# Whole instructions instead of quarters on GpSimd, in a two-layer mLSTM and attention trunk

## The chip, the cores and the metric

The kernel runs on 1 core of a Trainium2 chip. The core has five engines that work side by side: TensorE (PE, matrix products), VectorE (DVE), ScalarE (ACT), GpSimd (POOL) and SyncE (SP, which here only issues transfers). They meet only at semaphores. The metric is the device time of one execution in microseconds (us); lower is better.

## The reference, cut to what matters

Input and output are 1024 tokens of 1024 float32 numbers. Two layers are computed: layer 0 mixes tokens by an mLSTM with 4 heads in chunks of 128, layer 1 by differential attention with 8 heads. Each mixer and each MLP is preceded by an RMS norm and added to its input:

```
x = x + mixer_i(rmsnorm(x))              # i = 0: mLSTM, i = 1: differential attention
x = x + square(relu(rmsnorm(x) @ w_up)) @ w_down
out = rmsnorm(x)
# attention, per head, two maps c = 0, 1 with rotary q and k:
p_c = softmax(mask(q_c @ k_c.T * scale));  a = p_0 - lam * p_1;  o = a @ v
# rotary: concat(x1*cos - x2*sin, x2*cos + x1*sin)
```

## The kernel before, in words

Every product is done in three passes of a reduced-precision float32 (fp32r). A number v is split into a high part (v rounded to fp32r) and a low part (v minus the high part), and hi·hi + lo·hi + hi·lo are added up. So each weight panel of 1024x128 numbers must be split before PE may use it, and GpSimd does this for all panels of the mixers and of their output products: `split(g, slot, ...)` multiplies `w_raw` by ones into `w_hi` (the rounding), then subtracts into `w_lo`. There are 64 panels and two slots. The split of panel g starts when its weights are loaded and when PE has finished panel g-2 (`half_done`); PE waits for `w_split`, and SP waits for it before it loads the panel after next into the slot.

GpSimd has two more jobs of the same kind. `rotate(hd, j)` applies the rotary tables to q (j = 0) and k (j = 1) of an attention head: two products with sine and cosine tables and one sum over 128x1024 numbers. `split_early(layer)` splits finished mixer outputs (6 tiles of 128x1024 in layer 0, 7 in layer 1) while the last head is being computed, so that PE can begin the output product in between (`early_tile`). In these three functions each pass over 128x1024 numbers is issued as 4 instructions of 128x256 (the constant `PIECE` = 2 blocks of 128 columns). In the MLPs GpSimd runs `a_sums`, sums of weight blocks, each already one instruction of 128x1024; they are not touched.

The order of work on every engine is written out by hand. PE fills its waiting times in the mixers with the next panels' products: `feed(n)` issues n units of three matmuls between the steps of a head. In attention, step m of a head is: PE computes the scores (L1089, L1090), DVE adds the mask and takes the maximum for both maps (`mask_and_max`, L2148, L2149, both reading PSUM), ACT takes the exponentials (L1535), DVE combines the two maps (`combine`, L2160, which reads two SBUF tiles), and PE transposes the result (L1130) and multiplies it with v. Between the steps DVE also empties the panels' PSUM banks (`take`, L1649), and PE may overwrite a bank only after that. There are two banks, each used by every second half panel of 24 matmuls.

In the mLSTM DVE computes the gates of all heads in one long chain of small instructions (L1997 to L2017) while PE does the first panels. At each head's start it makes two tables (L2030, L2032), copies the new q, k and v (L2035, 128x4096) and prepares the decay matrix (L2039, L2043).

On the way from the first MLP to attention, SP issues the transfer that repeats q for the first head (`repeat_q`, L456, L459) behind a panel's load, and that load waits for the split of the panel before the last one (`load_panel`, L418).

Of the kernel before, what the change touches and what calls it, by code (L numbers as in the profile page):

```python
# [26 lines left out]
S = 1024  # L27
P = 128
NT = D // P
HALF = S // 2  # L30
# [8 lines left out]
NEG = -1e30  # L39


PIECE = 2
BATCHES = [-(-(m + 1) // 3) for m in range(NB)]
BEFORE = [sum(BATCHES[:m]) for m in range(NB)]
BATCH = sum(BATCHES)
# [60 lines left out]
def trunk(nc, x, ln_mix, ln_mlp, w_up, w_down, ln_f, m_w_in, m_b, m_norm, m_w_out,  # L106
          a_w_in, a_lam, a_norm, a_w_out, cos_t, sin_t, out):
    f32, f32r, i32 = mybir.dt.float32, mybir.dt.float32r, mybir.dt.int32
    ALU, ACT, AX = mybir.AluOpType, mybir.ActivationFunctionType, mybir.AxisListType
# [28 lines left out]
    def half_stage(layer, unit, s, q):  # L138

        return 2 * STAGES * UNITS * layer + 2 * stage_of(unit, s) + q + 1  # L140
# [66 lines left out]
    with ExitStack() as ctx:  # L207
        def sem(name):
            return ctx.enter_context(nc.semaphore(name))

        def sb(name, shape, dt=f32, stack=ctx):
            return stack.enter_context(nc.sbuf_tensor(name, shape, dt))


        h = sb("h", [P, NT, S])
# [7 lines left out]
        ones = sb("ones", [P, P])  # L223
# [13 lines left out]
        w_raw = sb("w_raw", [P, 2, NT, P])  # L237
        w_hi = sb("w_hi", [P, 2, NT, P], f32r)
        w_lo = sb("w_lo", [P, 2, NT, P], f32r)
# [34 lines left out]
        with ExitStack() as s:  # L274
# [8 lines left out]
            cosb = sb("cosb", [P, S], stack=s)  # L283
            sinb = sb("sinb", [P, S], stack=s)
# [74 lines left out]
        w_split = sem("w_split")  # L359
# [17 lines left out]
        y_early_hi, y_early = sem("y_early_hi"), sem("y_early")  # L377
# [6 lines left out]
        dve_chain, act_chain, pool_chain = sem("dve_chain"), sem("act_chain"), sem("pool_chain")  # L384
# [12 lines left out]
        pool_rot, rot_ready, qk_hi, qk_ready = sem("pool_rot"), sem("rot_ready"), sem("qk_hi"), sem("qk_ready")  # L397
# [232 lines left out]
        def _(pool):  # L630
# [16 lines left out]
            def split(g, slot, use, first=False):  # L647

                pool.wait_ge(w_ld[slot], 16 * use)
                if not first:  # L650
                    pool.wait_ge(half_done, 2 * (g - 1))
                if isinstance(g, int) and g in (G_MIX[1], G_MIX[1] + 1):

                    pool.wait_ge(hs_done, half_stage(0, UNITS - 1, 6, 0) - (1 if slot else 0))
                cuts = [slice(t, t + PIECE) for t in range(0, NT, PIECE)]
                for cut in cuts:
                    last = nc.gpsimd.tensor_tensor(w_hi[:, slot, cut], w_raw[:, slot, cut],  # L657
                                                   ones[:, :].unsqueeze(1).broadcast_to([P, PIECE, P]), ALU.mult)
                last.then_inc(pool_chain, 1)
                pool.wait_ge(pool_chain, 4 + g)  # L660
                for cut in cuts:
                    last = nc.gpsimd.tensor_tensor(w_lo[:, slot, cut], w_raw[:, slot, cut],  # L662
                                                   w_hi[:, slot, cut].bitcast(f32), ALU.subtract)
                last.then_inc(w_split, 1)


            split(1, 1, 1, first=True)

            for n in range(2, 2 * NT):
                pool.wait_ge(emit_hi, n + 1)  # L670
                if n >= 4:
                    pool.wait_ge(x_added, n - 3)
                nc.gpsimd.tensor_tensor(acc[:, n % 2], acc[:, n % 2], sq[:, n % 2], ALU.add).then_inc(x_added, 1)
            split(2, 0, 1)

            def pairs(start, end):

                with pool.Fori(0, (end - start) // 2) as i:
                    split(start + 2 * i, 1, i + (start + 1) // 2)
                    split(start + 1 + 2 * i, 0, i + (start + 1) // 2)  # L680

            def split_early(layer):

                hi, lo = one
                pool.wait_ge(half_done, 2 * G_OUT[layer])
                for t in range(EARLY[layer]):
                    if layer == 0:
                        pool.wait_ge(y_out, 4 * (t * P // MV + 1))
                    else:
                        pool.wait_ge(oy_out, 2 * (t + 1))  # L690
                    cuts = [(half, slice(c, c + PIECE * P)) for half in range(2) for c in range(0, HALF, PIECE * P)]
                    for half, cut in cuts:
                        y = h[:, t, half * HALF + cut.start:half * HALF + cut.stop]
                        last = nc.gpsimd.tensor_tensor(
                            hi[t // 4][:, half, t % 4, cut].rearrange("p (b c) -> p b c", c=P),
                            y.rearrange("p (b c) -> p b c", c=P),
                            ones[:, :].unsqueeze(1).broadcast_to([P, PIECE, P]), ALU.mult)
                    last.then_inc(y_early_hi, 1)
                    pool.wait_ge(y_early_hi, EARLY[0] * layer + t + 1)
                    for half, cut in cuts:  # L700
                        y = h[:, t, half * HALF + cut.start:half * HALF + cut.stop]
                        last = nc.gpsimd.tensor_tensor(lo[t // 4][:, half, t % 4, cut], y,
                                                       hi[t // 4][:, half, t % 4, cut].bitcast(f32), ALU.subtract)
                    last.then_inc(y_early, 1)

            def rotate(hd, j):

                x, partner = a_next[:, j], swap[:, j]
                pool.wait_ge(swapped[j], 64 * hd + 64)
                cuts = [slice(c, c + PIECE * P) for c in range(0, S, PIECE * P)]  # L710
                for y, table in ((partner, sinb), (x, cosb)):
                    for cut in cuts:
                        last = nc.gpsimd.tensor_tensor(y[:, cut], y[:, cut], table[:, cut], ALU.mult)
                    last.then_inc(pool_rot, 1)
                pool.wait_ge(pool_rot, 4 * hd + 2 * j + 2)
                for cut in cuts:
                    last = nc.gpsimd.tensor_tensor(x[:, cut], x[:, cut], partner[:, cut], ALU.add)
                last.then_inc(rot_ready, 1)

            def attention_head(i, a, more=True):  # L720

                g = 3 * (a + 1) + G_MIX[1]
                for p in range(3):
                    if p < 2:
                        rotate(2 * i + a, p)
                    if more:
                        split(g + p + 6 * i, (g + p) % 2, (g + p + 1) // 2 + 3 * i)
# [39 lines left out]
            for layer in range(2):  # L767
                g = G_OUT[layer]
                split(g, 1, (g + 1) // 2)
                split_early(layer)  # L770
                split(g + 1, 0, (g + 1) // 2)
                pairs(g + 2, g + 8)
                mlp(layer)
                if layer == 0:
                    g = G_MIX[1]
                    for p in range(3):
                        split(g + p, (g + p) % 2, (g + p + 1) // 2)
                    pool.wait_ge(cs_ld, 32)
                    with pool.Fori(0, AH // 2 - 1) as i:
                        for a in range(2):  # L780
                            attention_head(i, a)
                    attention_head(AH // 2 - 1, 0)
                    attention_head(AH // 2 - 1, 1, more=False)
# [1482 lines left out]
```

## Time and profile before

| | us |
|---|---|
| median of 3 runs | 2415.15 (2412.39 to 2415.46) |
| profiled execution: its own time | 2415.46 |
| profiled execution: span of the trace | 2413.7 |
| PE busy | 2289.1 (95%) |
| DVE busy | 1582.6 (66%) |
| POOL busy | 1039.8 (43%) |
| ACT busy | 886.9 (37%) |

All times below are in us from the span's start. The stages: first norm and gates' weights 0 to 57, mLSTM 57 to 434, its output product and the first MLP to 1146, panels of the first attention head to 1223, attention to 1676, output product and second MLP to 2391, output. In a quiet stretch PE starts a 128x512 matmul every 0.23 us, though each row shows 0.39 (they overlap), so one unit of three takes 0.68 and a half panel 5.4. How to read a row of the timeline: start, duration, engine, line, operation, output <- inputs, shapes, and in brackets the idle time before it with what ended it. Rows with x4 are several instructions merged, and their duration runs from the first one's start to the last one's end.

### The profile page before, as it was taken

Reading aid. Unit: us, or ns where it says so; the run is one execution under the profiler, and the core shown is the slowest. Engines: PE = TensorE matmul, PEld = TensorE weight load, DVE = VectorE, ACT = ScalarE, POOL = GpSimd, SP = SyncE. Lnnn points to the kernel's source line nnn. Section 1 sums busy time; section 2 is a strip of 40 time slices with the busy share of each in tenths; the row PEclk is TensorE's granted clock in tenths of the full one; section 3 lists DMA queues with packets and bytes.
Section 4 is the critical chain, followed back from the end, with each engine's and each line's share of the span. In section 5 each row is a group of like instructions: output and inputs, shape, how many; then the busy total and the mean of one; then the engine's idle time right before and its main releaser. Section 6 shows DMA issues by size and latency. Waiting matters only on the chain.

```text
span 2413.7 us, 28940 instructions
## 1 busy us (share of the span) xinstructions
PE 2289.1 (95%) x10601; PEld 1889.7 (78%) x10601; DVE 1582.6 (66%) x1956; ACT 886.9 (37%) x1471; POOL 1039.8 (43%) x962
## 2 busy tenths in 40 slices
PE   7999997899999999999879999988999999999998
PEld 5888885777788888888668888866877788888887
DVE  6533334469947849579357676776389849669396
ACT  3131122135334334345135544444144334343345
POOL 6544437443413233222666666667543232233230
PEclk8999999999999999999899999998999999999999
DMA  6111112246163342630422222222345262542601
GB/s 178 44 36 35 35 35 61 83 157 248 35 245 121 143 189 70 226 105 1 140 62 63 73 74 61 61 53 79 105 175 192 103 228 70 195 153 93 256 1 70
DMA packets 128835, 262.63 MB, mean 109 GB/s; under 512 B 7217, under 2 KB 81122, under 8 KB 121314
## 3 DMA queue, kind: packets, MB, share of 16 engines
q1 hardware_dynamic: 128290, 260.13, 31.9%
q8 instruction: 65, 1.06, 0.2%
q10 hardware_dynamic: 448, 1.18, 0.1%
q14 instruction: 32, 0.26, 0.0%
HBM read 202.56 MB, written 41.94 MB: 101 GB/s over the span
## 4 chain that ended last, share of the span: by engine, by line
PE 79%; DVE 11%; POOL 4%; ACT 2%; issue 2%; DMA 2%; SPq 0%; ACTq 0%; DVEq 0%; POOLq 0%
PE aps L916 9%; PE aps L920 9%; PE aps L918 9%; PE dps L816 5%; PE dps L818 5%; PE dps L817 5%; PE mps L920 3%; PE dps L920 3%; PE dps L916 3%; PE mps L916 3%; PE dps L918 3%; PE mps L918 3%; PE dps L798 2%; PE dps L800 2%; PE dps L799 2%
## 5 line engine op out<-in xcount | busy, mean ns | idle before, releaser
L657 POOL TENSOR_TENSOR w_hi<-w_raw,ones 128x256 fp32r<-128x256 f32 x256 | 210.7, 854 | 437.6 <-PE dps L818 250.6
L754 POOL TENSOR_TENSOR s_blk<-s_blk,a 128x1024 f32<-128x1024 f32 x32 | 93.6, 2926 | 408.7 <-DVE w_lo L1693 282.9
L916 PE MATMUL aps<-b_ring,w_hi 128*128 128x512 f32 x640 | 252.2, 394 | 15.3 <-issue 15.3
L816 PE MATMUL dps<-one_hi,w_hi 128*128 128x512 f32 x608 | 256.5, 422 | 0.0
L918 PE MATMUL aps<-b_ring,w_lo 128*128 128x512 f32 x640 | 251.1, 392 | 0.0
L920 PE MATMUL aps<-b_ring,w_hi 128*128 128x512 f32 x640 | 251.0, 392 | 0.0
L818 PE MATMUL dps<-one_lo,w_hi 128*128 128x512 f32 x608 | 238.5, 392 | 0.0
L817 PE MATMUL dps<-one_hi,w_lo 128*128 128x512 f32 x608 | 237.9, 391 | 0.0
L1711 DVE TENSOR_TENSOR b_ring<-h,b_ring 128x1024 fp32r<-128x1024 f32 x120 | 222.3, 1860 | 7.5 <-ACT b_ring L1325 7.5
L662 POOL TENSOR_TENSOR w_lo<-w_raw,w_hi 128x256 fp32r<-128x256 f32 x256 | 195.6, 795 | 5.0
L798 PE MATMUL dps<-one_hi,w_hi 128*128 128x512 f32 x384 | 152.8, 398 | 7.1 <-POOL w_lo L662 6.2
L916 PEld LDWEIGHTS aps<-b_ring,w_hi 128*128 128x128 f32 x640 | 121.5, 190 | 43.5 <-issue 18.4
L916 PE MATMUL aps<-b_ring,a_hi 128*128 128x512 f32 x384 | 150.1, 391 | 4.7 <-DVE b_ring L1711 3.8
L799 PE MATMUL dps<-one_hi,w_lo 128*128 128x512 f32 x384 | 151.4, 394 | 0.0
L800 PE MATMUL dps<-one_lo,w_hi 128*128 128x512 f32 x384 | 151.1, 394 | 0.0
L920 PE MATMUL aps<-b_ring,a_hi 128*128 128x512 f32 x384 | 149.5, 389 | 0.0
L918 PE MATMUL aps<-b_ring,a_lo 128*128 128x512 f32 x384 | 149.4, 389 | 0.0
L920 PEld LDWEIGHTS aps<-b_ring,w_hi 128*128 128x128 f32 x640 | 121.4, 190 | 25.7
L918 PEld LDWEIGHTS aps<-b_ring,w_lo 128*128 128x128 f32 x640 | 121.4, 190 | 25.2
L1325 ACT ACTIVATE b_ring<-h 128x1024 fp32r<-128x1024 f32 x112 | 116.4, 1048 | 57.9 <-DVE h L1746 42.6
L818 PEld LDWEIGHTS dps<-one_lo,w_hi 128*128 128x128 f32 x608 | 114.2, 188 | 25.5
L816 PEld LDWEIGHTS dps<-one_hi,w_hi 128*128 128x128 f32 x608 | 115.2, 189 | 18.5 <-issue 0.7
(292 smaller groups left out, 5570.2 us busy)
## 6 DMA issues: line engine op xcount, KB each, us to landing
b_ring<-xs SPq DMA_DIRECT2D x42, 2048.0 KB, 7.9
xs<-b_ring SPq DMA_DIRECT2D x14, 2048.0 KB, 7.5
a<-in_w_up SPq DMA_DIRECT2D x16, 1024.0 KB, 5.4
a<-in_w_down SPq DMA_DIRECT2D x16, 1024.0 KB, 7.6
w_raw<-in_mlstm_w_in SPq DMA_DIRECT2D x24, 512.0 KB, 4.0
w_raw<-in_diff_w_in SPq DMA_DIRECT2D x24, 512.0 KB, 3.8
hspill<-h SPq DMA_DIRECT2D x2, 4096.0 KB, 13.3
h<-hspill SPq DMA_DIRECT2D x16, 512.0 KB, 3.5
```

The source lines that it names most:

```text
L657: last = nc.gpsimd.tensor_tensor(w_hi[:, slot, cut], w_raw[:, slot, cut], ones[:, :].unsqueeze(1).broadcast_to([P, PIECE, P]), ALU.mult)
L662: last = nc.gpsimd.tensor_tensor(w_lo[:, slot, cut], w_raw[:, slot, cut], w_hi[:, slot, cut].bitcast(f32), ALU.subtract)
L798: nc.tensor.matmul(dps[:, half], w_hi[:, slot, k], rh, start=(k == 0), stop=False)
L799: nc.tensor.matmul(dps[:, half], w_lo[:, slot, k], rh, start=False, stop=False)
L800: last = nc.tensor.matmul(dps[:, half], w_hi[:, slot, k], rl, start=False, stop=(k == NT - 1))
L816: nc.tensor.matmul(dps[:, half], w_hi[:, slot, k], rh, start=(k == 0), stop=False)
L817: nc.tensor.matmul(dps[:, half], w_lo[:, slot, k], rh, start=False, stop=False)
L818: last = nc.tensor.matmul(dps[:, half], w_hi[:, slot, k], rl, start=False, stop=(k == NT - 1))
L916: nc.tensor.matmul(to[:, n], wh, ring[:, 0, k], start=new and k == 0, stop=False, skip_group_check=not new)
L918: nc.tensor.matmul(to[:, n], wl, ring[:, 0, k], start=False, stop=False, skip_group_check=not new)
L920: last = nc.tensor.matmul(to[:, n], wh, ring[:, 1, k], start=False, stop=(k == 3), skip_group_check=not new)
L1711: last = nc.vector.tensor_tensor(lo, tiles_of(src, q), hi, ALU.subtract)
```

## The change

`PIECE` and the loops over pieces are gone. `split`, `split_early` and `rotate` issue each pass over 128x1024 numbers as one instruction. The arithmetic, the semaphores and their values, the order and all other engines' programs stay as they are.

```diff
@@ split
-                cuts = [slice(t, t + PIECE) for t in range(0, NT, PIECE)]
-                for cut in cuts:
-                    last = nc.gpsimd.tensor_tensor(w_hi[:, slot, cut], w_raw[:, slot, cut],
-                                                   ones[:, :].unsqueeze(1).broadcast_to([P, PIECE, P]), ALU.mult)
-                last.then_inc(pool_chain, 1)
+                nc.gpsimd.tensor_tensor(w_hi[:, slot], w_raw[:, slot],
+                                        ones[:, :].unsqueeze(1).broadcast_to([P, NT, P]),
+                                        ALU.mult).then_inc(pool_chain, 1)
                 pool.wait_ge(pool_chain, 4 + g)
...
+                nc.gpsimd.tensor_tensor(w_lo[:, slot], w_raw[:, slot], w_hi[:, slot].bitcast(f32),
+                                        ALU.subtract).then_inc(w_split, 1)
@@ split_early
...
+                    nc.gpsimd.tensor_tensor(rows_[0], rows_[1],
+                                            ones[:, :].unsqueeze(1).unsqueeze(1).broadcast_to([P, 2, 4, P]),
+                                            ALU.mult).then_inc(y_early_hi, 1)
                     pool.wait_ge(y_early_hi, EARLY[0] * layer + t + 1)
...
+                    nc.gpsimd.tensor_tensor(rows_[2], rows_[1], rows_[0].bitcast(f32),
+                                            ALU.subtract).then_inc(y_early, 1)
@@ rotate
-                for y, table in ((partner, sinb), (x, cosb)):
-                    for cut in cuts:
-                        last = nc.gpsimd.tensor_tensor(y[:, cut], y[:, cut], table[:, cut], ALU.mult)
-                    last.then_inc(pool_rot, 1)
+                nc.gpsimd.tensor_tensor(partner, partner, sinb[:, :], ALU.mult).then_inc(pool_rot, 1)
+                nc.gpsimd.tensor_tensor(x, x, cosb[:, :], ALU.mult).then_inc(pool_rot, 1)
                 pool.wait_ge(pool_rot, 4 * hd + 2 * j + 2)
...
+                nc.gpsimd.tensor_tensor(x, x, partner, ALU.add).then_inc(rot_ready, 1)
```

GpSimd's queue in the attention loop, one head's first rotation and the split behind it, before the change:

```order
L713 TENSOR_TENSOR swap<-swap,sinb 128x256 [waits q_swapped]
L713 TENSOR_TENSOR swap<-swap,sinb 128x256 x3
L713 TENSOR_TENSOR a_next<-a_next,cosb 128x256 x4
L717 TENSOR_TENSOR a_next<-a_next,swap 128x256 [waits pool_rot]
L717 TENSOR_TENSOR a_next<-a_next,swap 128x256 x3
L657 TENSOR_TENSOR w_hi<-w_raw,ones 128x256 [waits half_done,w_ld0]
L657 TENSOR_TENSOR w_hi<-w_raw,ones 128x256 x3
L662 TENSOR_TENSOR w_lo<-w_raw,w_hi 128x256 [waits pool_chain]
L662 TENSOR_TENSOR w_lo<-w_raw,w_hi 128x256 x3
```

The same place in the changed kernel, at its first head:

```order
L700 TENSOR_TENSOR swap<-swap,sinb 128x1024 [waits q_swapped]
L701 TENSOR_TENSOR a_next<-a_next,cosb 128x1024
L702 ISA
L703 TENSOR_TENSOR a_next<-a_next,swap 128x1024 [waits pool_rot]
L648 ISA
L650 ISA [waits w_ld0]
L654 TENSOR_TENSOR w_hi<-w_raw,ones 128x1024 [waits half_done]
L657 REGISTER_ALU
L658 TENSOR_TENSOR w_lo<-w_raw,w_hi 128x1024 [waits pool_chain]
```

Twenty instructions of 128x256 became five of 128x1024, with the same waits ahead of the same passes (the rows ISA and REGISTER_ALU set registers for the loop). The order of passes did not move.

In the last head of the mLSTM, GpSimd splits finished tiles; one tile of the six, before and then after:

```order
L694 TENSOR_TENSOR one_hi<-h,ones 128x256 [waits y_out]
L694 TENSOR_TENSOR one_hi<-h,ones 128x256 x3
L702 TENSOR_TENSOR one_lo<-h,one_hi 128x256 [waits y_early_hi]
L702 TENSOR_TENSOR one_lo<-h,one_hi 128x256 x3
```

```order
L689 TENSOR_TENSOR one_hi<-h,ones 128x2x512 [waits y_out]
L693 TENSOR_TENSOR one_lo<-h,one_hi 128x2x512 [waits y_early_hi]
```

Here too eight instructions became two, and each tile is still handed to PE by one semaphore step.

## Rows read from the trace of the kernel before

**Rows 1.** Windows by stage: length, busy time (instructions) per engine, PE clock, DMA.
```profile
57.00:434.00 377.00, 356.18 (x1632) 290.37 (x1631) 160.28 (x331) 87.44 (x220) 185.38 (x240) 0.98 0.15 41
1223.00:1676.00 453.00, 429.18 (x2378) 361.63 (x2378) 317.43 (x691) 222.48 (x612) 295.69 (x384) 0.97 0.24 62
```
**Rows 2.** Waits of PE, whole span: waiter <- releaser: total, times, longest.
```profile
PE aps L1089 <- DMA q_lo<-q_lo: 11.9, 1, 11.9
...
PE dps L798 <- POOL w_lo L662: 6.2, 2, 5.0
```
**Rows 3.** Groups by form, POOL: busy, mean ns | idle before, releasers.
```profile
L657 POOL TENSOR_TENSOR w_hi<-w_raw,ones 128x256 fp32r<-128x256 f32 x256 | 210.7, 854 | 437.6 <-PE dps L818 250.6 <-PE dps L800 75.4 <-PE aps L920 39.9
```
**Rows 4.** Timeline of POOL, first rotation: four quarters in a row.
```profile
1184.26 2.85 POOL L713 TENSOR_TENSOR a_next<-a_next,cosb 128x256 f32<-128x256 f32 x4
```
**Rows 5.** Timeline of POOL in the first MLP: whole instructions, free and held.
```profile
610.27 2.40 POOL L754 TENSOR_TENSOR s_blk<-s_blk,a 128x1024 f32<-128x1024 f32 x1 [5.70 <-DVE w_lo L1693]
...
1092.46 3.32 POOL L759 TENSOR_TENSOR s_blk<-a12d,s_blk 128x1024 f32<-128x1024 f32 x1 [3.43 <-DVE w_lo L1693]
```
**Rows 6.** Timeline of DVE beside it: one held instruction, two free ones.
```profile
1093.44 3.43 DVE L1711 TENSOR_TENSOR b_ring<-h,b_ring 128x1024 fp32r<-128x1024 f32 x1
...
1099.06 2.35 DVE L1711 TENSOR_TENSOR b_ring<-h,b_ring 128x1024 fp32r<-128x1024 f32 x2
```
**Rows 7.** Groups by form, DVE: the mask, read from PSUM.
```profile
L2148 DVE TENSOR_TENSOR aps<-aps,mask_qk 128x128 f32<-128x128 f32 x128 | 37.3, 292 | 31.1 <-PE aps L1090 30.8
```
**Rows 8.** Timeline of DVE in one attention head: two combines of eight.
```profile
1352.30 0.92 DVE L2160 SCALAR_TENSOR_TENSOR ee<-ee,small 128x384 f32<-128x384 f32 x1
...
1363.94 0.89 DVE L2160 SCALAR_TENSOR_TENSOR ee<-ee,small 128x640 f32<-128x640 f32 x1
```
**Rows 9.** Timeline of POOL in the same stretch.
```profile
1352.06 3.13 POOL L717 TENSOR_TENSOR a_next<-a_next,swap 128x256 f32<-128x256 f32 x4
1355.16 2.81 POOL L657 TENSOR_TENSOR w_hi<-w_raw,ones 128x256 fp32r<-128x256 f32 x4
...
1363.42 3.40 POOL L713 TENSOR_TENSOR swap<-swap,sinb 128x256 f32<-128x256 f32 x4 [2.22 <-DMA swap<-a_next]
```
**Rows 10.** Timeline of PE: the transposes that wait for these combines.
```profile
1354.73 0.49 PE L1130 MATMUL mps<-ident,ee 128*128 128x128 f32 x3
...
1366.11 0.60 PE L1130 MATMUL mps<-ident,ee 128*128 128x128 f32 x4
```
**Rows 11.** Timeline of DVE, gates: two of eight iterations, then the bank's emptying.
```profile
74.66 0.87 DVE L2013 TENSOR_SCALAR nm<-m_cur,mst 4x128 f32<-4x128 f32 x1
...
79.27 0.69 DVE L1649 SCALAR_TENSOR_TENSOR m_next<-dps,rstd_bc 128x512 f32<-128x512 f32 x1
...
81.06 0.28 DVE L2013 TENSOR_SCALAR nm<-m_cur,mst 4x128 f32<-4x128 f32 x1
```
**Rows 12.** Timeline of PE: the half panel that needs that bank.
```profile
80.01 0.50 PE L798 MATMUL dps<-one_hi,w_hi 128*128 128x512 f32 x1
```
**Rows 13.** Timeline of DVE and of POOL at the start of mLSTM's last head.
```profile
378.75 0.74 DVE L2030 TENSOR_SCALAR relu<-acc,ident 128x1024 f32<-128x1024 f32 x1
...
380.82 2.54 DVE L2035 COPY m_cur<-m_next 128x4096 f32<-128x4096 f32 x1
...
378.18 5.76 POOL L694 TENSOR_TENSOR one_hi<-h,ones 128x256 fp32r<-128x256 f32 x4 [5.08 <-PE dps L818]
```
**Rows 14.** Chain of waits, whole span and just before attention.
```profile
12.66 4.00 POOL w_hi L657 x4
...
1206.01 4.76 POOL w_hi L657 x4
...
1216.47 6.53 DMA q_lo<-q_lo
```
**Rows 15.** Waits of PE, 1572 to 1680, the last two attention heads.
```profile
PE mps L1130 <- DVE ee L2160: 3.2, 5, 1.6
```
**Rows 16.** Timeline of DVE there: one combine.
```profile
1641.28 1.30 DVE L2160 SCALAR_TENSOR_TENSOR ee<-ee,small 128x512 f32<-128x512 f32 x1
```

More of the change, by code:

```diff
@@ L39 @@
 NEG = -1e30
-PIECE = 2
 BATCHES = [-(-(m + 1) // 3) for m in range(NB)]
@@ L654, in split @@
                     pool.wait_ge(hs_done, half_stage(0, UNITS - 1, 6, 0) - (1 if slot else 0))
-                cuts = [slice(t, t + PIECE) for t in range(0, NT, PIECE)]
-                for cut in cuts:
-                    last = nc.gpsimd.tensor_tensor(w_hi[:, slot, cut], w_raw[:, slot, cut],
-                                                   ones[:, :].unsqueeze(1).broadcast_to([P, PIECE, P]), ALU.mult)
-                last.then_inc(pool_chain, 1)
+                nc.gpsimd.tensor_tensor(w_hi[:, slot], w_raw[:, slot],
+                                        ones[:, :].unsqueeze(1).broadcast_to([P, NT, P]),
+                                        ALU.mult).then_inc(pool_chain, 1)
                 pool.wait_ge(pool_chain, 4 + g)
-                for cut in cuts:
-                    last = nc.gpsimd.tensor_tensor(w_lo[:, slot, cut], w_raw[:, slot, cut],
-                                                   w_hi[:, slot, cut].bitcast(f32), ALU.subtract)
-                last.then_inc(w_split, 1)
+                nc.gpsimd.tensor_tensor(w_lo[:, slot], w_raw[:, slot], w_hi[:, slot].bitcast(f32),
+                                        ALU.subtract).then_inc(w_split, 1)
             split(1, 1, 1, first=True)
@@ L690, in split_early @@
                         pool.wait_ge(oy_out, 2 * (t + 1))
[L691 to L698, printed above, removed]
-                    pool.wait_ge(y_early_hi, EARLY[0] * layer + t + 1)
[L700 to L704, printed above, removed]
+                    rows_ = [v.rearrange("p a (b c) -> p a b c", c=P) for v in
+                             (hi[t // 4][:, :, t % 4], h[:, t].rearrange("p (a b) -> p a b", a=2),
+                              lo[t // 4][:, :, t % 4])]
+                    nc.gpsimd.tensor_tensor(rows_[0], rows_[1],
+                                            ones[:, :].unsqueeze(1).unsqueeze(1).broadcast_to([P, 2, 4, P]),
+                                            ALU.mult).then_inc(y_early_hi, 1)
+                    pool.wait_ge(y_early_hi, EARLY[0] * layer + t + 1)
+                    nc.gpsimd.tensor_tensor(rows_[2], rows_[1], rows_[0].bitcast(f32),
+                                            ALU.subtract).then_inc(y_early, 1)
             def rotate(hd, j):
@@ L709, in rotate @@
                 pool.wait_ge(swapped[j], 64 * hd + 64)
-                cuts = [slice(c, c + PIECE * P) for c in range(0, S, PIECE * P)]
-                for y, table in ((partner, sinb), (x, cosb)):
-                    for cut in cuts:
-                        last = nc.gpsimd.tensor_tensor(y[:, cut], y[:, cut], table[:, cut], ALU.mult)
-                    last.then_inc(pool_rot, 1)
+                nc.gpsimd.tensor_tensor(partner, partner, sinb[:, :], ALU.mult).then_inc(pool_rot, 1)
+                nc.gpsimd.tensor_tensor(x, x, cosb[:, :], ALU.mult).then_inc(pool_rot, 1)
                 pool.wait_ge(pool_rot, 4 * hd + 2 * j + 2)
-                for cut in cuts:
-                    last = nc.gpsimd.tensor_tensor(x[:, cut], x[:, cut], partner[:, cut], ALU.add)
-                last.then_inc(rot_ready, 1)
+                nc.gpsimd.tensor_tensor(x, x, partner, ALU.add).then_inc(rot_ready, 1)
             def attention_head(i, a, more=True):
```

## The prediction

> **What bounds the kernel now.** I read the windows by stage first, then PE's waits, then the timelines of POOL and DVE side by side. PE is busy for 356 of 377 us in the mLSTM and for 429 of 453 in attention [rows 1]: the end is set by PE almost everywhere, and time can come only from a wait of PE that goes or is added. PE's waits are few [rows 2]: 11.9 us before the first scores, for a transfer, and 6.2 for two weight splits. POOL is behind PE nearly always: the 256 quarters of the high part stand behind 437.6 us of idle time, most of it waiting for PE [rows 3]. So a faster POOL is worth little, except where the chain of waits runs through it [rows 14]. What counts more is what POOL does to DVE.
>
> **What one pass costs POOL.** Four quarters in a row take 2.85 us [rows 4], one whole instruction of the same 1024 columns 2.40 when nothing holds it [rows 5]. A pass gets 0.45 shorter. There are 202 of them (64 panels with 2 passes, 13 tiles with 2, 16 rotations with 3), 91 us of POOL's 1040. The mean duration of a quarter, 854 ns [rows 3], would make that 4 x 0.854 - 2.40 = 1.0 per pass, but it contains time in which a quarter was held; I go by the row of four. The Trainium skill (Perfetto Trace Analysis, GPSIMD Engine Instruction) says that a GpSimd row's own length is unreliable and that the spacing of consecutive starts should be used; this trace agrees, 0.85 against about 0.70. With 1.0 instead of 0.45 the gain below at the start of attention would be 12 us instead of 5.4.
>
> **What one pass costs DVE.** In the MLP, where POOL's instructions are whole already, a DVE instruction that starts 1.0 us into a POOL instruction of 3.32 [rows 5] takes 3.43 us, where the same one takes 2.35 for two in a row when POOL rests [rows 6]. 1092.46 + 3.32 = 1095.78, and DVE ends at 1096.87, one free duration later: it waited for POOL's whole instruction. The reverse is in the same row: POOL's 3.32 is 0.9 above the free 2.40. DVE's mask, which reads PSUM and one SBUF tile, is not held at all (292 ns on average over 128) [rows 7]. So the instructions that count are those of DVE with two SBUF inputs and its plain copies and scalings of SBUF. Today they wait for a quarter, 0.7 at most and 0.35 on average; after the change for a pass, up to 2.3 and 1.15 on average. As far as these rows show, the two engines take turns: whoever asked first goes next. A chain of many small DVE instructions therefore loses a turn of POOL per instruction today, and the sum over a whole split stays about the same; it is the single DVE instruction with a near deadline that loses. The Trainium skill (SBUF — State Buffer, Who interferes with whom) states it as an exclusive lock held for the whole instruction, which speaks against this change; by that rule alone, with no turn won back, every combine would pay as in the third rival.
>
> **Part by part.** The places are replayed from the rows: each engine keeps its order, a DVE instruction of the held kind waits for the running pass, and a POOL pass waits for the running DVE instruction.
>
> (a) First split. It is on the chain at 12.66 [rows 14]; two passes give -0.9. Bounds 0 and -0.9.
>
> (b) Gates, 64 to 97. DVE's eight iterations of four small instructions run beside three splits: L2013 takes 0.87 beside POOL and 0.28 alone [rows 11]. The bank is emptied at 79.27 to 79.96 and PE needs it at 80.01 [rows 11, 12]: no slack. Replayed, the iterations before it lose 0.6 in the first split, and the second split's two passes of 2.3 come at the wrong side of two instructions more: the bank is empty at about 82.1, and PE stops for 2.1. The next such point (around 91, where PE already waits) costs 1.2 more. +3.3; bounds 0 and +6 (a pass more at each place).
>
> (c) Starts of the first three mLSTM heads. L2030 comes half a us after POOL's pass and waits for it, L2032 for the next; behind them stand the copy of 2.54 and the decay matrix that PE waits for. PE has four units of other work there, which covers most: +0.5 each, +1.5. Bounds 0 and +3.
>
> (d) Last mLSTM head. POOL runs 12 passes without a pause. L2030 (378.75), L2032 and the copy (380.82) [rows 13] each lose a turn to a pass: the copy starts at about 386.2 instead of 380.8, +5.3 for the first step. Today PE later waits for the last two tiles of POOL anyway; these come some 3 us earlier (12 x 0.45 less what the copy's 2.5 us of holding moves), so 4 of the 5.3 are swallowed. Then L2053 in each of eight steps waits 1.1 on average with 0.9 of slack: +2; and POOL is through before the head's last chain of small instructions: -1.3. Sum +2; bounds -3 and +6.
>
> (e) The split after it. PE waits 6.2 - 5.0 = 1.2 [rows 2]; two passes earlier: -0.7. Bounds 0 and -0.9.
>
> (f) From the first MLP to attention. From 1175.3 POOL runs 12 passes in a row (two panels, q, a panel, k, a panel); SP can issue the repeat of q only when the last of them is done, at 1213.6, and the 6.53 us of the transfer end in PE's wait of 11.9 [rows 14, 2]. 12 x 0.45 = -5.4. Before it, DVE's splits of the MLP's last outputs run beside two panels' splits and end in front of a PE wait; with longer turns DVE is held while ACT cannot run ahead, +1.5. Sum -3.9; bounds -5.4 and 0. This is the largest gain.
>
> (g) Six full attention heads and the first. Of eight combines per head two are near a deadline and beside a pass. At 1352.30 the combine takes 0.92 and ends at 1353.22, PE needs it at 1354.73: 1.5 of slack [rows 8, 10]. After the change the combines before it have each lost a turn and DVE comes about 0.8 late, just behind the start of the panel's pass (1355.16 today [rows 9], 1352.9 then); it is held to 1355.1 and PE waits 1.05. At 1363.94 the slack is 1366.11 - 1364.83 = 1.3, and the k rotation starts 0.5 before it [rows 8 to 10]; held to 1366.1, it makes PE wait 0.9. Each is a close race (0.2 to 0.5 us decide), so I count half: +1.0 per head, +7 in all. Bounds 0 and +16 (both always, and one more of 0.4). What is late next is absorbed: PE-paced panels' splits start later too.
>
> (h) The last head but one has fewer filling units and PE waits for combines already [rows 15]; its combines at 1580, 1595 and 1601 stand beside passes with no slack. Three times 0.8 more, and 0.6 behind: +3. Bounds 0 and +6.
>
> (i) The last head has no filling but early tiles. The combine at 1641.28 takes 1.30 [rows 16] where some 0.75 are free (an estimate from 1.2 per 1024 columns and a fixed part); seven such steps, and POOL works without pause. Five lose 0.8 more each; the last two are free since POOL is done earlier: +3.5 after 0.5 off. Bounds 0 and +7.
>
> In the output products and the MLPs nothing changes: in the former a bank has 5.4 us of slack against two turns of 2.3.
>
> Sum: -0.9 + 3.3 + 1.5 + 2 - 0.7 - 3.9 + 7 + 3 + 3.5 = +14.8. The profiled execution took 2415.46 (span 2413.7), 0.3 above the median of the runs, 2415.15; so about 2430.
>
> **Rivals.**
> - Faster: the slack of the deadlines covers the longer turns, because POOL's passes, being shorter in sum, drift out of the way of the combines. Then only (a), (e), (f) and POOL's part of (d) (-3) are left: -0.9 - 0.7 - 5.4 - 3 = -10, 2405. For it: PE's waits for combines are only 3.2 us today [rows 15]. Against it: the bank at 80.01 has none. It decides if the added hold on DVE in front of PE's needs stays below 10 us in sum.
> - No difference: the sum of POOL's turns is the same, gains of (f) cancel against (b), (c) and the last heads, and the races of (g) are won: -4 + 5 + 3 = +4 at most, 2417.
> - All races lost: each of 64 combines pays a mean of 0.8 more in the two thirds of the time in which POOL is busy (296 of 453) [rows 1], 64 x 0.8 x 0.66 = 34, less (f): 2445. Against it: slack of 1 to 3 us at most steps.
> - The hold lasts only a part of an instruction and POOL yields in between. Then it is the first rival; rows 5 and 6 speak against it.
>
> **Chances.** Forecast 0.55, faster 0.12, no difference 0.18, all races lost 0.15. From no change a measurement can tell about 0.2%, 5 us: faster is below 2410, slower above 2420. Slower 0.55 and 0.15 and a little of the third: 0.72. Same 0.16, faster 0.12. The forecast's own terms reach from 2418 to 2442; the range reaches toward both rivals: 2411 to 2447.
>
> **What would show it.** Right: POOL has rows of 2.4 where there were four; DVE's L2160 with maxima of 3 us; L2030 or L2035 at the last mLSTM head with 2 to 3 us more; PE's wait for L1649 near 80; PE's wait for the q_lo transfer shorter by 4; PE's waits for L2160, 3.2 in the last two heads now, growing to some 15 us over all attention. Wrong: L2160 grows but PE's row of waits does not, or attention from first scores to the end stays at 453 us; or passes that take 2.8.

## The result, and the profile after

| | before | after |
|---|---|---|
| median, us | 2415.15 | 2426.4 (2425.79 to 2429.71) |
| profiled execution, span | 2415.46, 2413.7 | 2426.3, 2424.5 |
| PE busy | 2289.1 | 2292.3 |
| DVE busy | 1582.6 | 1671.7 |
| POOL busy | 1039.8 | 921.1 |

The ratio is 1.0051, 95% interval 1.0037 to 1.0066: slower, by 9 to 16 us. POOL has 119 us less work, DVE is 89 us longer occupied by the same instructions (a row of DVE that is held by POOL is recorded longer, with its waiting in it), and PE waits longer.

PE's waits over the whole span after the change, four of the rows (waiter, releaser, total us, times, longest):

```profile
PE aps L1098 <- DVE sq L2154: 20.7, 2, 17.8
PE aps L1074 <- DMA q_lo<-q_lo: 12.8, 1, 12.8
PE mps L1115 <- DVE ee L2145: 10.1, 16, 1.9
PE dps L783 <- DVE m_next L1634: 3.5, 2, 1.9
```

The lines moved: L2154 is L2169 of before, L1098 is L1113, L2145 L2160, L1634 L1649, L1074 L1089. The first row stands out. PE waited for that multiplication, the end of `head_norm` (the norm of a head's output, a chain of small DVE instructions), twice before too. The row of before:

```profile
PE aps L1113 <- DVE sq L2169: 9.5, 2, 6.6
```

POOL's and DVE's groups by form, after (busy, mean ns | idle before):

```profile
L654 POOL TENSOR_TENSOR w_hi<-w_raw,ones 128x1024 fp32r<-128x1024 f32 x64 | 165.6, 2587 | 533.1 <-PE dps L803 288.1 <-PE dps L785 95.3 <-DMA w_raw<-in_diff_w_out 40.4
...
L2133 DVE TENSOR_TENSOR aps<-aps,mask_qk 128x128 f32<-128x128 f32 x128 | 37.2, 290 | 25.5 <-PE aps L1075 25.3
L2145 DVE SCALAR_TENSOR_TENSOR ee<-ee,small 128x768 f32<-128x768 f32 x8 | 15.2, 1899 | 0.3
...
L2145 DVE SCALAR_TENSOR_TENSOR ee<-ee,small 128x640 f32<-128x640 f32 x8 | 8.8, 1106 | 0.3
L2145 DVE SCALAR_TENSOR_TENSOR ee<-ee,small 128x384 f32<-128x384 f32 x8 | 6.5, 812 | 0.3
```

A pass is one row, 2.4 when free and 2.59 on average with the held ones, where four quarters took 2.85 [rows 4]. The mask, which reads PSUM, is as fast as before [rows 7]; the combines are not.

**Where the time went.** Both programs run the same 10601 matmuls in the same order, so the k-th of one trace can be set against the k-th of the other. The table gives by how many us each stretch is longer than in the trace of before (times of before; + is slower), for the change and for eight of the twelve experiments below. The first row counts from the first matmul, and the last row ends at the last one.

| stretch | after | e1 | e2 | e3 | e4 | e12 | e11 | e6 | e9 |
|---|---|---|---|---|---|---|---|---|---|
| 0 to 74, start | -3.5 | -0.8 | -0.4 | -2.7 | -1.2 | -0.4 | -2.3 | -3.3 | -1.6 |
| 74 to 93, gates | +2.7 | +2.6 | -0.9 | +2.6 | +2.6 | -0.9 | +2.1 | 0 | -0.9 |
| 93 to 372, three mLSTM heads | +0.3 | +0.3 | 0 | +0.3 | +0.3 | 0 | +0.1 | 0 | +0.1 |
| 372 to 433, last mLSTM head | +0.5 | +0.2 | -0.7 | -0.8 | -0.7 | +0.8 | -2.8 | 0 | -2.1 |
| 433 to 1100, one split (at 448) | -2.3 | +0.2 | -1.5 | -1.4 | -1.7 | -2.2 | +0.1 | 0 | -0.4 |
| 1100 to 1160, end of the first MLP | +2.0 | +2.0 | 0 | +2.1 | +1.5 | 0 | +0.6 | 0 | 0 |
| 1160 to 1223, up to the first scores | -5.6 | -5.4 | +0.5 | -6.7 | -2.0 | -3.2 | -3.6 | -4.7 | -5.6 |
| 1223 to 1603, full attention heads | +6.1 | +2.1 | -0.7 | +4.4 | +0.8 | +5.3 | 0 | +0.2 | +0.9 |
| 1603 to 1616 | 0 | +1.6 | 0 | 0 | 0 | 0 | 0 | +1.6 | +1.6 |
| 1616 to 1627, head norm | +11.3 | 0 | +11.3 | -4.9 | +11.3 | 0 | +4.8 | 0 | -4.9 |
| 1627 to 1690, last head | +2.1 | +3.2 | +2.8 | +5.0 | +1.9 | +3.5 | +1.4 | -0.2 | +1.7 |
| 1690 to the last matmul, nothing changed | -3.0 | -2.4 | -2.4 | -2.9 | -2.4 | -2.5 | -2.6 | -2.4 | -2.4 |

The stretches in which little or nothing was changed show how far one trace can be trusted: 2 to 3 us each. Part of this lies in the trace of before: the last row reads -2.4 to -3.0 in every column. The start reads -0.8 to -3.5 with the first split whole, and in the old form -0.4 (e2, e12) but also -2.2 (e5). The row before the head norm's is 0 or +1.6, also without a change in it; its cause was not looked for. The head norm row is of another kind: it takes only the values -4.9, 0, +4.8 and +11.3.

**The head norm.** DVE after the change; eleven instructions of 8 columns and the multiplication stand in a row, here six of them:

```profile
1618.71 1.83 DVE L2151 TENSOR_SCALAR small<-small 128x8 f32<-128x8 f32 x1
...
1620.78 2.19 DVE L1615 TENSOR_TENSOR small<-small 128x8 f32<-128x8 f32 x1
1623.00 2.26 DVE L1616 SCALAR_TENSOR_TENSOR small<-small 128x8 f32<-128x8 f32 x1
1625.30 0.17 DVE L1617 SCALAR_TENSOR_TENSOR small<-small 128x8 f32<-128x8 f32 x1
1625.50 2.19 DVE L1615 TENSOR_TENSOR small<-small 128x8 f32<-128x8 f32 x1
...
1634.94 3.25 DVE L2154 TENSOR_TENSOR sq<-sq,small 128x1024 f32<-128x1024 f32 x1
```

POOL beside it, in `split_early` of layer 1:

```profile
1620.59 2.35 POOL L693 TENSOR_TENSOR one_lo<-h,one_hi 128x1024 fp32r<-128x1024 f32 x1
1622.90 2.33 POOL L689 TENSOR_TENSOR one_hi<-h,ones 128x1024 fp32r<-128x1024 f32 x1
1625.32 2.35 POOL L693 TENSOR_TENSOR one_lo<-h,one_hi 128x1024 fp32r<-128x1024 f32 x1
```

And PE, which has nothing else to do there:

```profile
1638.25 1.97 PE L1098 MATMUL aps<-ident,sq 128*128 128x128 f32 x8 [17.84 <-DVE sq L2154]
```

An instruction that needs 0.17 takes 2.2: it starts when a pass has just begun and ends when the pass ends. Then POOL takes its next turn (one instruction of its queue), and the chain waits for that, at once or after one free instruction of 0.17. So 8 of the 12 instructions are held. In the kernel before the same chain met quarters, and 10 of the 12 were held, each for one quarter at most:

```profile
1620.22 0.65 DVE L1631 SCALAR_TENSOR_TENSOR small<-small 128x8 f32<-128x8 f32 x1
...
1625.12 1.70 DVE L2169 TENSOR_TENSOR sq<-sq,small 128x1024 f32<-128x1024 f32 x1
```

**Gates.** Two of DVE's small instructions fall on the two passes of one split, 2.47 and 2.45 where 0.28 is free [rows 11]; the bank is emptied late, and PE waits 1.63, and 1.9 at the next such place.

```profile
71.12 2.40 POOL L654 TENSOR_TENSOR w_hi<-w_raw,ones 128x1024 fp32r<-128x1024 f32 x1 [6.00 <-PE dps L785]
71.14 2.47 DVE L1998 TENSOR_SCALAR nm<-m_cur,mst 4x128 f32<-4x128 f32 x1
...
73.63 2.45 DVE L2000 TENSOR_SCALAR nm<-m_cur 4x128 f32<-4x128 f32 x1
...
77.37 0.69 DVE L1634 SCALAR_TENSOR_TENSOR m_next<-dps,rstd_bc 128x512 f32<-128x512 f32 x1
...
78.11 0.50 PE L783 MATMUL dps<-one_hi,w_hi 128*128 128x512 f32 x1 [1.63 <-DVE m_next L1634]
```

**Full attention heads.** In three of the six full heads (waits of PE at 1251, 1425 and 1484) the combine of 768 columns asks at the moment when the last pass of a rotation begins, and loses. DVE's row, and POOL's:

```profile
1250.83 3.24 DVE L2145 SCALAR_TENSOR_TENSOR ee<-ee,small 128x768 f32<-128x768 f32 x1
...
1250.87 2.39 POOL L703 TENSOR_TENSOR a_next<-a_next,swap 128x1024 f32<-128x1024 f32 x1
```

It is 2.2 late, of which PE notices 1.2 to 1.3. Two heads later the same pair stands almost as close, and the combine wins; now POOL is held:

```profile
1367.60 1.02 DVE L2145 SCALAR_TENSOR_TENSOR ee<-ee,small 128x768 f32<-128x768 f32 x1
...
1367.66 3.21 POOL L703 TENSOR_TENSOR a_next<-a_next,swap 128x1024 f32<-128x1024 f32 x1
```

So the row of the full heads is made of races. The same code lost this one three times here (+6.1), twice in e3's trace (+4.4) and once in e1's (+2.1), each time for 1.4 in the table. The combine of 640 columns, which the prediction named, lost to the rotation before it in one head here, at 1303 (2.65, PE +0.6); in that head the one of 768 was safe. The combines that grew most on average, those of 128 columns (0.40 to 1.90) and of 512 (0.91 to 2.14), mostly have slack: PE hardly waits for them in the full heads.

**Last mLSTM head.** DVE's two tables and its copy each lose a turn, and POOL is held by the copy in its turn:

```profile
378.17 2.34 DVE L2015 TENSOR_SCALAR relu<-acc,ident 128x1024 f32<-128x1024 f32 x1
380.43 2.83 DVE L2017 TENSOR_SCALAR cb<-acc,ident 128x1024 f32<-128x1024 f32 x1
...
383.45 4.16 DVE L2020 COPY m_cur<-m_next 128x4096 f32<-128x4096 f32 x1
...
385.53 4.28 POOL L693 TENSOR_TENSOR one_lo<-h,one_hi 128x1024 fp32r<-128x1024 f32 x1
```

PE is 6.3 behind at 400 and 0.5 at 433: the waits of 3.9 for POOL's tiles are gone, and that for the head's last chain fell from 6.3 to 4.9, since POOL is done by then.

### The profile page after: what moved, and what is told of

It reads as the page before. It is cut to its first block, busy times and chain, and to the rows that moved or that the text cites. A ratio compares the mean times of both kernels' runs of the same rounds, so it can differ in the third digit from the quotient of the medians.

```text
span 2424.5 us, 28334 instructions
## 1 busy us (share of the span) xinstructions
PE 2292.3 (95%) x10601; PEld 1888.8 (78%) x10601; DVE 1671.7 (69%) x1956; ACT 889.1 (37%) x1471; POOL 921.1 (38%) x356
## 4 chain that ended last, share of the span: by engine, by line
PE 79%; DVE 13%; issue 3%; ACT 3%; DMA 1%; POOL 1%; SPq 0%; ACTq 0%; DVEq 0%; POOLq 0%
PE aps L901 9%; PE aps L903 9%; PE aps L905 9%; PE dps L803 5%; PE dps L801 5%; PE dps L802 5%; PE mps L903 3%; PE dps L903 3%; PE mps L905 3%; PE dps L901 3%; PE dps L905 3%; PE mps L901 3%; PE dps L783 3%; PE dps L784 2%; PE dps L785 2%
## 5 line engine op out<-in xcount | busy, mean ns | idle before, releaser
L654 POOL TENSOR_TENSOR w_hi<-w_raw,ones 128x1024 fp32r<-128x1024 f32 x64 | 165.6, 2587 | 533.1 <-PE dps L803 288.1
L658 POOL TENSOR_TENSOR w_lo<-w_raw,w_hi 128x1024 fp32r<-128x1024 f32 x64 | 160.9, 2514 | 5.0
L1678 DVE TENSOR_TENSOR w_lo<-s_blk,w_hi 128x1024 fp32r<-128x1024 f32 x68 | 93.8, 1380 | 55.6 <-ACT w_hi L1276 55.6
```

What stands on the lines that cost most here:

```text
L654: nc.gpsimd.tensor_tensor(w_hi[:, slot], w_raw[:, slot], ones[:, :].unsqueeze(1).broadcast_to([P, NT, P]), ALU.mult).then_inc(pool_chain, 1)
L658: nc.gpsimd.tensor_tensor(w_lo[:, slot], w_raw[:, slot], w_hi[:, slot].bitcast(f32), ALU.subtract).then_inc(w_split, 1)
```

## The experiments

Before each, what was expected; each was timed against the kernel before on its own chip.

**e1: split_early in quarters, the rest whole.**

```diff
 # changed kernel, split_early
-nc.gpsimd.tensor_tensor(rows_[0], rows_[1], ...)
+for half, cut in cuts:   # 4 instructions of 128x256, as before
```

> The changed kernel with only split_early back in quarters. Theory (turns): DVE's chain of ten small instructions in the head norm at the start of the last head meets a whole pass of split_early at nearly every instruction, and PE's wait for L2154, 17.8 us, is the sum of these turns. With quarters there each turn is at most 0.7, the wait is 6.6 again as in the kernel before, and the time falls by 11 to 12: 2426.4 - 11.5 = 2415. Rival (combines): what was lost is the combines' lateness in the six full heads and the gates, and the 17.8 stands in place of waits that come later anyway (POOL's last tiles, the end of the head); then the wait shrinks but the time stays within 3 us of 2426.

Measured 2419.5, ratio 1.002 (1.001 to 1.003). The wait is 6.6 again and the head norm row 0, as the theory says. But the time fell by 7, not 11.5. The table doesn't settle where the rest is: against the change's trace the start, the stretch from 433 to 1100, the row before the head norm's and the last head are 2.7, 2.5, 1.6 and 1.1 longer, of which only the last head has instructions of the edit in it, and the full heads are 4.0 shorter, by two lost races fewer.

**e2: only split_early whole.**

```diff
 # kernel before, split_early: one instruction per pass
```

> The kernel before with only split_early in whole instructions; split and rotate stay in quarters. Theory (turns): PE's wait for the head norm grows from 6.6 to about 18, the last mLSTM head costs 1 more, nothing else moves: 2415.2 + 11.3 + 0.8 = 2427, as slow as the whole change although only 26 of 202 passes changed. Rival (combines): about 2416.

Measured 2424.8, ratio 1.004 (1.0026 to 1.0053); the wait is 17.8, the row +11.3. 26 passes of 202 make most of the slowdown.

**e3: all whole, but POOL waits for the head norm.**

```diff
                 pool.wait_ge(half_done, 2 * G_OUT[layer])
+                if layer == 1:
+                    pool.wait_ge(on_ready, AH - 1)
```

> The changed kernel, all passes whole, but GpSimd starts the early tiles of layer 1 only when the head norm of the last head but one is done. Theory (turns): beside an idle GpSimd the chain of ten small instructions takes 0.17 to 0.3 each and 0.9 to 1.2 for the multiplication, about 3 us instead of 20; PE's wait of 17.8 falls to 1 to 2. Of these 16 some 3 to 5 come back, because the combines of the last head now stand beside whole passes from its start and because the tiles come 3 us later: 2426.4 - 16 + 4 = 2414. Rival (not the turns but the work: DVE or the chain itself is slow there): the wait stays above 6.6 as in the kernel before and the time above 2417. Second rival: the tiles come too late, PE waits for y_early instead, 5 us or more, 2420.

Measured 2411.0, ratio 0.9983 (0.9974 to 0.9992): faster than before, 15 less than the change. The same instructions, alone:

```profile
1616.99 0.17 DVE L1617 TENSOR_TENSOR small<-small 128x8 f32<-128x8 f32 x1
...
1618.79 1.22 DVE L2156 TENSOR_TENSOR sq<-sq,small 128x1024 f32<-128x1024 f32 x1
```

The chain takes 3.4 us instead of 19.5, PE's wait 1.8 instead of 17.8. So the work was never slow; it was held. The tiles were in time (no wait of PE for POOL there), and the last head came out 3 longer (5.0 against 2.1), where its combines now stand beside whole passes.

**e4: rotate in quarters, the rest whole; e12: only rotate whole.**

```diff
 # e4: the changed kernel with the old rotate; e12: the kernel before with the new one
```

> The changed kernel with only rotate back in quarters; the panels' splits stay whole. It divides the +7 of the attention heads and the -4 before them. Three of the twelve passes in front of the first scores for q and three for k are rotations: 6 x 0.45 = 2.7 of the gain go back. If the rotations are what hold the combines (the race at the step with 640 columns), PE's waits for L2145 between 1223 and 1600, 6.0 in 12 now and 1.9 in 8 before, fall to 3 to 4 and the stretch is 3 shorter: total 2426 again (2424 to 2428). If the panels' passes hold them, the waits stay at 5 to 6 and the total is 2428 to 2429. The wait of 17.8 stays in both.

> The kernel before with only rotate in whole instructions. With rotate in quarters and everything else whole the stretch of the full attention heads (1226 to 1603) cost 0.8; with all whole it cost 6.1, 4.4 and 2.1 in three traces. Theory (it is the rotations that hold the combines): the stretch costs 2 to 6 here too, the scores come 2.7 earlier: 2414.2 + 1.3 = 2415.5 (2413 to 2418). Rival (it takes both, or the scatter between traces is all there is): the stretch costs under 1, 2412.

Measured 2426.7 for e4 (ratio 1.0048, 1.0034 to 1.0062) and 2415.9 for e12 (1.0013, 1.0004 to 1.0022). PE's waits for combines from 1218 to 1605, first e4, then e12:

```profile
PE mps L1121 <- DVE ee L2151: 3.1, 9, 1.1
```

```profile
PE mps L1125 <- DVE ee L2155: 4.8, 16, 0.7
```

The full heads cost 0.8 with whole splits alone and 5.3 with whole rotations alone. These are two single traces of a row that scatters by 4 with the same code, but their rows agree: in e12 the combine of 640 columns takes 2.40 to 2.85 in all six full heads, and in e4 it takes 0.89 and that of 768 at most 1.64. The rotations hold the combines; the prediction's race of 640 columns is the one that e12 loses, for 0.4 to 0.8 each, and with whole splits as well its moment shifts and that of 768 is lost instead. In total e12 is 1 to 5 us slower than before. The gain before the scores divides into -2.0 and -3.2, six passes each (six times 0.45 is 2.7).

**e8: split_early in halves, the rest in quarters.** A turn between the two known lengths.

```diff
 # kernel before, split_early only
-PIECE (2 blocks)
+4 blocks, 512 columns an instruction
```

> The kernel before with split_early alone in halves (512 columns an instruction) instead of quarters. Theory (one turn of GpSimd for each small instruction): a turn is about 1.25 us instead of 0.68, nine instructions are held, and PE's wait for L2169, 6.6 with quarters and about 18 with whole passes, becomes 6.6 + 9 x 0.57 = 11.7; the time 2414.6 + 5 = 2420. Rival (a fixed number of passes is lost, or the sum of turns is the same whatever their length): the wait stays at 7 to 8, 2415, or jumps to 17, 2425.

The wait is 11.4 (expected 11.7) and the head norm row +4.8. DVE's row and POOL's (2 halves):

```profile
1618.96 1.19 DVE L1630 TENSOR_TENSOR small<-small 128x8 f32<-128x8 f32 x1
```

```profile
1618.86 2.48 POOL L694 TENSOR_TENSOR one_hi<-h,ones 128x512 fp32r<-128x512 f32 x2
```

The time did not follow: 2413.4, ratio 0.9995 (0.9986 to 1.0004), not 2420, a miss. The last mLSTM head gave 2.4 back, since its tiles come earlier and PE's 3.9 of waiting for them are gone. The other 2.5 should then have stayed; the interval ends at +1 us. In this trace they are met by -1.3 from 433 to 1100 and small terms, and whether that is more than scatter is open. With e2 and e3 this is the measure of the cause:

| POOL beside the chain | chain, us | held instructions | lost by each | PE's wait |
|---|---|---|---|---|
| none (e3) | 3.4 | 0 | | 1.8 |
| quarters (before) | 8.2 | 10 | 0.48 | 6.6 |
| halves (e8) | 13.05 | 10 | 0.97 | 11.4 |
| whole (after) | 19.5 | 8 | 2.0 | 17.8 |

**e5: all in quarters, POOL waits for the head norm.** The edit is e3's, in the kernel before.

> The kernel before, all passes in quarters, but GpSimd starts the early tiles of layer 1 only when the head norm of the last head but one is done. Theory (turns): the 6.6 us of PE's wait for L2169 are turns too, of a quarter each; without them the chain takes about 2.7 and the wait falls to 1 to 2; 1 of the 5 comes back at the combines: 2414.6 - 4 = 2410.5. Rival (the chain's own time): the wait stays at 5 to 6.6 and the time at 2414 to 2415.

Measured 2416.8, ratio 1.001 (1.0001 to 1.0019): no gain, a miss. The head norm row is -4.9 as expected, but POOL begins the tiles some 4 us later in the program and PE comes 5 us earlier, and now waits for them:

```profile
1663.16 0.79 PE L946 MATMUL dps<-one_hi,w_hi 128*128 128x512 f32 x1 [5.57 <-POOL one_lo L704]
```

Fourteen passes in quarters leave no room for the delay; whole passes (e3) did. It is what I had put down as second rival for e3, and not for this run.

**e6: whole only where POOL is on the chain of waits.**

```diff
-            split(1, 1, 1, first=True)
+            split(1, 1, 1, first=True, piece_=NT)
-                split(g + 1, 0, (g + 1) // 2)
+                split(g + 1, 0, (g + 1) // 2, piece_=PIECE if layer else NT)
-                        split(g + p, (g + p) % 2, (g + p + 1) // 2)
+                        split(g + p, (g + p) % 2, (g + p + 1) // 2, piece_=NT if p == 2 else PIECE)
+                    attention_head(0, 0, piece_=NT)   # out of the loop
```

> The kernel before with whole passes only where GpSimd is on the chain of waits: the first panel's split, the panel after the last mLSTM head, the third panel of attention and the first head's rotations and panels. All others in quarters. Theory: the gain of the stretch from the first MLP to the scores stays (5.5 of it at the scores in the whole change), 0.7 and 0.9 come from the other two, and none of the places where whole passes cost (gates 2.7, end of the MLP 2, attention heads 2 to 6, head norm 11) is touched: 2414.6 - 6.5 = 2408. Rival (the gain is only there because the loads and PE come earlier too, or it is returned by a longer wait for q_lo): 2412 to 2415.

Measured 2408.0, ratio 0.9971 (0.996 to 0.9981), as forecast. -4.7 before the scores, and none of the costs.

**e7: e5 and e6 together.**

> Both of the two before: whole passes on the chain, quarters elsewhere, and the early tiles of layer 1 after the head norm. Theory: the two gains lie in different stretches and add: 2414.6 - 6.5 - 4 = 2404. Rival (the clock or the end of the last head gives part of it back): 2407 to 2410.

Measured 2411.1, ratio 0.9985 (0.9976 to 0.9994), not 2404: 3 above e6 on the same chip (their intervals just overlap). The wait of 5.6 is e5's.

**e9: e6, both split_early in halves, and POOL waits for the head norm; e10: e6 with only layer 0's in halves.**

```diff
-                split_early(layer)
+                split_early(layer, 4)                    # e9, with e3's wait
+                split_early(layer, 2 if layer else 4)    # e10, without it
```

> Whole passes on the chain of waits as in e6, split_early of both layers in halves (2.5 a pass instead of 2.85), layer 1's held back until the head norm is done, all else in quarters. In e7 the hold won 6 to 9 us at the norm and lost 7.7 again where PE waited for the held tiles (5.6 and 0.8); fourteen passes in halves end 14 x 0.4 = 5.6 earlier, so that wait should be about gone. Theory: 2408.0 (e6) - 5 (hold) - 2.6 (last mLSTM head, as in e8) + 1.5 (combines beside halves) = 2402. Rival (tiles still late: the wait for one_lo stays at 4 or more, or the combines take it): 2406 to 2409.

> The same without the hold and with layer 1's early tiles in quarters: whole passes on the chain, layer 0's early tiles in halves. Theory: the wait for the head norm is 6.6 again, the last mLSTM head keeps its -2.6: 2408.0 - 2.6 = 2405.5; the difference to the one before is what the hold is worth. Rival (the -2.6 of that head in e8 is scatter): 2408.

Measured 2402.1 (2398.32 to 2403.0) for e9, ratio 0.995 (0.9936 to 0.9964), and 2404.3 for e10, ratio 0.9965 (0.9951 to 0.9979). e9 is 11 to 12 us faster than the kernel before and 24 faster than the change. Its waits between 1600 and 1680 hold no POOL row any more:

```profile
PE aps L1118 <- DVE sq L2174: 4.7, 2, 2.9
...
PE mps L1135 <- DVE ee L2165: 2.1, 3, 1.4
```

e9 and e10 differ by 2.2, and their intervals overlap: that the hold adds to e10 is likely and not shown.

**e11: every pass in halves.**

> The kernel before with PIECE = 4: every pass in two instructions of 512 columns. Theory (a turn of 1.25 instead of 0.68 or 2.35 for each small instruction of DVE, a pass of 2.5 instead of 2.85 or 2.4): wait for the head norm +4.8 as in e8, gates +0.8 (2.7 with whole passes), end of the MLP +0.7 (2), attention heads +1, scores -4.2, last mLSTM head -2.6, first splits -1: 2414.2 - 1 = 2413. Rival (costs in proportion to the number of instructions saved, two thirds of the whole change's +11): 2421.

Measured 2414.1, ratio 1.0005 (0.9996 to 1.0014), no difference from before: the cost depends on the length of the turn at each deadline, not on how many instructions were saved.

## Why the prediction was right in sum, and where it was wrong

The forecast was 2430, and 2426.4 came out, slower, inside the range. Its mechanism, that DVE waits for POOL's whole instruction, is what the runs show. Its distribution is not, and that the sum came near is luck: the largest single cost was left out of it.

- **One pass**: 2.85 to 2.40 in POOL's free rows, 0.45 less, as worked out. POOL's busy time fell by 119, not by 91; it counts the time in which passes are held as well.
- **(a)** -0.9 can't be read: the start scatters by more than that.
- **(b) Gates**, +3.3: +2.7, waits of 1.63 and 1.9 for the predicted 2.1 and 1.2. All four kernels with whole splits in the table show 2.6 to 2.7, e11 in halves 2.1.
- **(c)** +1.5: +0.3. PE's other work there covered nearly all.
- **(d)** +2: +0.5, and -0.7 to -0.8 in e2, e3 and e4. The loss at the start was bigger than written (6.3 instead of 5.3) and was swallowed almost whole.
- **(e)** -0.7: can't be read. PE's wait at 448 fell by 1.4, but it did so in e5 and e8 too, where that split is in quarters, and in e6, where it is whole, by 0.2.
- **(f)** -5.4 and +1.5: -5.6 (-4.7 to -6.7 in the kernels that are whole there) and +2.0. The largest gain stands as worked out. In the rows it stands elsewhere than forecast: PE's wait for the q_lo transfer did not get shorter by 4, it went from 11.9 to 12.8, and the one for a split just before it went from 5.0 to 0.6. The two belong together: in e5, where nothing was changed so far, the latter is 2.5 shorter too, but the stretch only 0.3. (The twelve passes are one panel, q, a panel, k and a panel; "two panels" in the prediction is a slip that does not enter the sum.)
- **(g)** +7: +6.7 up to 1565 in this trace; the row that ends at 1603 is +6.1 here, +4.4 and +2.1 in e3 and e1, whose code there is the same. That each is a close race was right; which one, was not: that of 384 columns grew shorter (0.95 to 0.81), that of 640 was lost once, and the one of 768, which meets the rotation's third pass, three times. That the size fits is luck too.
- **(h)** +3: -0.6 between 1565 and 1616.
- **(i)** +3.5: +2.1, within the scatter of that stretch (-0.2 and 3.5 in e6 and e10, whose code there is that of before).
- **Left out: the head norm**, +11.3, more than any term of the sum. It stands in the stretch of (h) and (i), for which the prediction had 6.5 in all, and put them on the combines.

The step that failed is the sentence "A chain of many small DVE instructions therefore loses a turn of POOL per instruction today, and the sum over a whole split stays about the same; it is the single DVE instruction with a near deadline that loses". Its first half is nearly exact (10 of 12 instructions before). The second holds only if POOL runs out of work inside the chain. `split_early` of layer 1 has 14 passes in a row, the chain used 8 of them, so every held instruction paid a full turn: 8 x 2.0 - 10 x 0.48 = 11.2. The chain also has the nearest deadline of the kernel, since PE already waited 6.6 for it; that row (9.5, 2, 6.6, above) was at hand in the waits of before, and I read only the combines in the same view [rows 15]. Priced at nothing, this chain cost 11.3.

How the sum came near: from the gates to the last head, without the stretch from 433 to 1100, the table adds up to +19.4. Without the head norm that is +8.1, where the prediction's terms there, all but (a) and (e), had +16.4. So the named terms were 8 too large and the one left out was 11, and the start and the other stretches, 8.8 shorter in this pair of traces, did the rest; the runs say 9 to 16. One sum of the rivals has a slip as well: no difference plus 4 is 2419, not 2417, which moves nothing else.

Of the signs for it, the rows of 2.4, the combines of 3.2, the held tables and copy (1.6 more for L2030 and for L2035, not 2 to 3) and PE's wait near 80 came; the shorter wait for q_lo did not, as said. None of the signs against it came: no passes of 2.8, and no growing combines without growing waits of PE (4.2 to 10.1 over all attention, where some 15 had been named). The windows of the mLSTM and of attention, the latter now from 1217 to 1689.6:

```profile
57.00:434.00 377.00, 357.31 (x1616) 289.96 (x1616) 178.94 (x322) 85.33 (x219) 149.66 (x60) 0.97 0.14 40
1217.00:1689.60 472.60, 431.66 (x2378) 361.98 (x2378) 352.65 (x691) 224.50 (x612) 242.90 (x96) 0.96 0.23 60
```

Attention grew from 453 to 472.6, with nearly the same busy time of PE, 431.7 against 429.2 [rows 1]. DVE's busy time in the mLSTM grew from 160 to 179.

## What to carry to other kernels

Where two engines take turns, the length of one's instruction is a price that the other pays for each instruction of a dependent chain (for 8 to 10 of 12 here), as long as the first one's queue does not run dry. So look for the chain of tiny instructions that a third engine waits for, and see whether the long work beside it can start after it; here that was worth 15 us to the changed kernel. Choose the size of instructions place by place: whole where GpSimd itself is waited for, halves or quarters beside VectorE's deadlines. A delay of the long work needs slack of its own, which e5 and e7 did not have.

## What the runs showed of the hardware

- VectorE and GpSimd do not meet at semaphores alone, as the section on the chip has it: the 0.17 that took 2.2 waited for none.
- A free pass of 1024 columns takes 2.40 whole, about 2.50 in two instructions (2.47 to 2.55 in e11) and 2.85 in four. The second cut costs 0.35 for two instructions more, the first only 0.10.
- Who goes first isn't safely readable from the starts: the combine of 1250.83 is recorded 0.04 before the pass of 1250.87 and still waited for all of it, 3.24 against the 1.02 of the same instruction at 1367.60, which is recorded 0.06 before its pass and was free. The Trainium skill (SBUF — State Buffer, Who interferes with whom) says that whoever issues first keeps the shared ports for the whole instruction; the traces agree with the whole instruction, and show in addition that a chain loses its place after each of its instructions (8 of 12 held by whole passes, 10 of 12 by quarters).
- The long wait of PE was followed by a stretch at the lower clock. After, the 18 us of waiting (granted clock 0.66) and the 15 behind them (0.50):

```profile
1620.00:1638.00 18.00, 0.41 (x4) 0.21 (x2) 17.62 (x12) 1.06 (x2) 17.68 (x9) 0.66 0.30 87
1638.00:1653.00 15.00, 10.58 (x32) 7.29 (x32) 12.45 (x27) 4.90 (x18) 14.76 (x7) 0.50 0.35 105
```

0.50 of full speed is the lower of the two levels, 1.2 GHz. Before, with a wait of 6.6, the 15 us behind it (1627 to 1642) already had 0.59. What the difference costs is not separated from the rest of the last head (+2.1).
